# Computing each weight strip's low half in two GpSimd operations of 128x512 instead of one of 128x1024

## What is computed

```
h = h + mixed @ w_out                              # mixed: hyena long convolution and mLSTM
h = h + cross_attention(rms_norm(h), rms_norm(mem), wq, wk, wv, wo)
h = h + square(relu(rms_norm(h) @ ff_w1)) @ ff_w2
...
b_a, c_a, x_a, x_b, g_b, ga, gb = split(rmsnorm(x) @ w_in)
y_a = b_a * causal_conv(c_a * x_a);  y_b = rg_lru(causal_conv(x_b)) * gelu(g_b)
x = x + (sigmoid(ga) * (y_a @ w_out_a) + sigmoid(gb) * (y_b @ w_out_b)) @ w_o
x = x + (silu(h @ w_gate) * (h @ w_up)) @ w_down;  return rmsnorm(x)
```

## Time and profile before

| | |
|---|---|
| median of 3 runs | 1944.73 us (1944.62 to 1947.07) |
| the profiled execution: time, span | 1949.02 us, 1947.2 us |
| busy: PE, DVE, POOL, ACT | 1776.1, 1055.6, 753.2, 584.5 us |
| mean granted TensorE clock | 0.956 of full speed |
| weight strips | 302, 512 KB each |

### The profile page before, as it was taken

One profiled execution on the slowest core, in us unless ns is written; L12 is line 12 of the kernel. 1 busy time (PEld: TensorE's weight loads), 2 busy tenths in 40 slices (PEclk: granted clock), 3 DMA queues, 4 the chain that ended last, 5 costly groups with the idle time before them and its releaser, 6 DMA issues.

```text
span 1947.2 us, 21967 instructions
## 1 busy us (share of the span) xinstructions
PE 1776.1 (91%) x7718; PEld 1433.0 (74%) x7718; DVE 1055.6 (54%) x1379; ACT 584.5 (30%) x709; POOL 753.2 (39%) x312
## 2 busy tenths in 40 slices
PE   6799988975889998999999789898999999999996
PEld 4677876654667677888888577676888888888885
DVE  5751487879782566233248867575533463133137
ACT  2322332332212221111111254646433233122221
POOL 3432441113333143444444244444544444444442
PEclk9899998987899998999999899999999999999998
DMA  4232220110222022222222122223222222222222
GB/s 156 87 109 76 96 78 33 44 44 32 87 97 76 33 92 71 97 97 97 97 97 97 65 87 93 102 86 104 91 97 97 97 95 96 94 95 96 97 97 97
DMA packets 47694, 169.28 MB, mean 87 GB/s; under 512 B 5204, under 2 KB 5204, under 8 KB 47320
## 3 DMA queue, kind: packets, MB, share of 16 engines
q1 hardware_dynamic: 44640, 160.45, 23.6%
q10 hardware_dynamic: 3000, 8.09, 1.2%
HBM read 166.43 MB, written 2.10 MB: 87 GB/s over the span
## 4 chain that ended last, share of the span: by engine, by line
issue 31%; PE 29%; POOL 13%; DVE 1%; POOLq 0%; ACT 0%; DVEq 0%
POOL m_w_lo L433 13%; PE ps L465 10%; PE ps L467 10%; PE ps L466 10%; DVE m_h L1917 0%; DVE m_s L1187 0%; POOLq L441 0%; POOLq L439 0%; POOL m_QL L453 0%; DVE m_qs L1559 0%; PE ps L493 0%; DVE m_qs L1561 0%; DVE m_s L1894 0%; DVE m_ftmp L1551 0%; DVE m_ftmp L1549 0%
## 5 line engine op out<-in xcount | busy, mean ns | idle before, releaser
L433 POOL TENSOR_TENSOR m_w_lo<-m_raw,m_w_hi 128x1024 fp32r<-128x1024 f32 x302 | 738.8, 2450 | 1119.1 <-ACT m_w_hi L875 1119.1
L875 ACT ACTIVATE m_w_hi<-m_raw 128x1024 fp32r<-128x1024 f32 x302 | 317.7, 1056 | 761.4 <-DMA m_raw<-in_strips 757.6
L465 PE MATMUL ps<-m_XH,m_w_hi 128*128 128x512 f32 x1160 | 474.4, 409 | 36.6 <-POOL m_w_lo L433 22.5
L466 PE MATMUL ps<-m_XL,m_w_hi 128*128 128x512 f32 x1160 | 458.8, 396 | 0.0
L467 PE MATMUL ps<-m_XH,m_w_lo 128*128 128x512 f32 x1160 | 458.6, 395 | 0.0
L465 PEld LDWEIGHTS ps<-m_XH,m_w_hi 128*128 128x128 f32 x1160 | 222.7, 192 | 101.0 <-POOL m_w_lo L433 27.2
L466 PEld LDWEIGHTS ps<-m_XL,m_w_hi 128*128 128x128 f32 x1160 | 223.0, 192 | 47.6 <-issue 2.7
L467 PEld LDWEIGHTS ps<-m_XH,m_w_lo 128*128 128x128 f32 x1160 | 222.0, 191 | 47.9
L465 PE MATMUL ps<-m_FH,m_w_hi 128*128 128x512 f32 x432 | 168.9, 391 | 3.3 <-DVE m_FL L1180 3.2
L466 PE MATMUL ps<-m_FL,m_w_hi 128*128 128x512 f32 x432 | 168.6, 390 | 0.0
L467 PE MATMUL ps<-m_FH,m_w_lo 128*128 128x512 f32 x432 | 168.5, 390 | 0.0
(11 more groups left out here) (311 smaller groups left out, 2295.8 us busy)
## 6 DMA issues: line engine op xcount, KB each, us to landing
m_raw<-in_strips SPq DMA_DIRECT2D x302, 512.0 KB, 3.2
m_x_in<-in_x ACTq DMA_DIRECT2D x8, 256.0 KB, 4.6
m_x_res<-in_x ACTq DMA_DIRECT2D x1, 2048.0 KB, 8.0
out<-m_h SPq DMA_DIRECT2D x8, 256.0 KB, 2.1
m_memf<-in_mem ACTq DMA_DIRECT2D x1, 1024.0 KB, 10.4
m_decay<-in_decay ACTq DMA_DIRECT2D x1, 1024.0 KB, 15.1
m_w<-in_w ACTq DMA_DIRECT2D x1, 512.0 KB, 13.6
m_skip<-in_skip ACTq DMA_DIRECT2D x1, 512.0 KB, 3.9
```

Of the source, the lines that this page charges most:

```text
L433: nc.gpsimd.tensor_tensor(w_lo[:, c], raw[:, c], f(w_hi[:, c]), ALU.subtract).then_inc(lo_ready, 1)
L465: pe.matmul(dst, w_hi[:, c], xh, start=first, stop=False)
L466: pe.matmul(dst, w_hi[:, c], xl, start=False, stop=False)
L875: act.activation(w_hi[:, c], raw[:, c], ACT.Copy).then_inc(hi_ready, 1)
```

## The change

`low` runs over the two halves of a strip, and each half adds one to `lo_ready`. Every wait on `lo_ready` on TensorE is doubled, so that TensorE still starts a strip when the whole of it is there. ACT, DVE and SP are unchanged, and so are the six operations on `QL`.

```diff
             def low(slot):
-                c = slice(slot * STRIP, (slot + 1) * STRIP)
-                nc.gpsimd.tensor_tensor(w_lo[:, c], raw[:, c], f(w_hi[:, c]), ALU.subtract).then_inc(lo_ready, 1)
+                for part in range(2):
+                    c = slice(slot * STRIP + part * (STRIP // 2), slot * STRIP + (part + 1) * (STRIP // 2))
+                    nc.gpsimd.tensor_tensor(w_lo[:, c], raw[:, c], f(w_hi[:, c]), ALU.subtract).then_inc(lo_ready, 1)
...
             def strip(n, slot, bank, xh, xl, kt=KT, taken=None, needs=None, counts=None, width=T):
 
-                pe.wait_ge(lo_ready, n + 1)
+                pe.wait_ge(lo_ready, (n + 1) * 2)
...
                     n = v * 6 + 5
-                    pe.wait_ge(lo_ready, i * 12 + (S_IN + n + 1))
+                    pe.wait_ge(lo_ready, (i * 12 + (S_IN + n + 1)) * 2)
```

More of the change, by code:

```diff
@@ L716, in _ @@
             for u in range(4):
-                pe.wait_ge(lo_ready, S_WOUT + u + 1)
+                pe.wait_ge(lo_ready, (S_WOUT + u + 1) * 2)
                 for k in range(4, KT):
```

## The result

The changed kernel takes 1912.18 us (median of 4 runs, 1910.67 to 1914.59), the kernel before 1944.67 in runs on the same chip. The ratio is 0.9831, with a 95% interval of 0.9814 to 0.9848: 1.7% faster, 32.5 us. The forecast was 1933 (11.6 us less), with a range from 1928 to 1948. The sign was right and the gain was almost three times the forecast one.

What follows compares the result with a forecast made beforehand. PE, busy 1776.1 of 1947.2 us, was taken as the bound, not POOL; the change halves POOL's port lock on DVE. Terms summed to -11.55 from the median 1944.73, giving 1933.2 (forecast 1933), range 1928 to 1948.

Steps and rivals of the forecast that it cites:

- Rival C: Everywhere: POOL keeps the port between halves, so DVE waits as before and d longer; 1949.3 us, chance 0.12.
- Rival B: Gains are given back as POOL's second half takes the port first; two places remain, 1943 us, chance 0.19.
- Rival D: in_turn: strip C's low sets the turn, which grows by 0.59 us; 1944 to 1949 us, chance 0.07.
- d: Fixed extra time of two halves over one whole POOL operation: taken as 0.12 us, bounds 0 to 0.25.
- The taps at 112.71: PE's 4.56 us wait for L1256, held by the second of two low; released after its first half: -1.0 us.
- the three mLSTM units: L1422 released 1.1 us earlier, PSUM reads next, about 0.3 lost on L1440: 3 x 0.8 = -2.4 us.
- the Hyena block of `L1561`: A half-length block of L1561 ahead of PE's 2.81 us wait at 460.04: -1.1 us.
- the residual: After w_out, 541 to 580: L1197 released earlier at three places followed by PSUM reads: 3 x 0.9 = -2.7 us.
- the last residual: Before PE's 3.98 us wait at 1073.97: last tile's L1180 released 1.1 earlier, and 0.3 before that: -1.4 us.
- the first hidden chunk: 740 to 765: L1178 held less, mostly given back to L1180, inside PE's 3.18 us wait: -1.7 us.
- the second half delays strip C's `low` by 0.6: in_turn replay: taps let go 1.1 us earlier, but the turn gains only 0.08, 8 turns: -0.6 us.
- What it gives back, place by place: List of gains from hand replays of held DVE operations; from -0.6 us in in_turn to -2.7 after w_out.

Runs made afterwards that it cites:

- Experiment 5: Kernel before, with one strip in six of each in_turn turn in halves, beside the first pair of taps: 1944.01 us, ratio 0.9973.
- experiment 6: Kernel before, with only the fourth strip of each in_turn turn in halves, beside the scan: 1952.38 us, ratio 1.0009.
- experiment 4: Changed kernel, but TensorE starts a strip at the first half's signal and waits for the second ahead of the fifth block: 1915.23 us, ratio 0.9845.
- Experiment 7: Kernel before, whole operations, with 64 extra throwaway matmuls on TensorE in the Hyena part's wait between its two orders: 1987.75 us, ratio 1.0200.
- experiment 1: Kernel before, with halves only for the 48 strips of in_turn, whole operations elsewhere: 1931.76 us, ratio 0.9911.
- hi first: TensorE does w_hi matmuls first, waiting for POOL only before a strip's last eight: four parts 1889.04 us against 1882.36, eight parts 1859.51 against 1870.61.

## Why the prediction was wrong in size

**What bounds the kernel, and the mechanism: right.** The two stretches in which TensorE is never short moved by +0.2 and +1.5 us. One detail of the readings is off: a held operation does not end when POOL's does, but later by about its own work, 0.55 us for the tap (1181.40 against 1180.85) and 1.1 for the scan. Rival C, a port kept between the halves, has fallen with the first row of DVE: 2.45 for the pair of taps. Rival B, everything given back, fell with the result; the give-back exists, at the places named (`L1852` 1.60, and `L1718` and `L1720`, six blocks of 1.2 as foretold), but it is not the rule. Rival D has fallen too: the turn got shorter. Rival B was close at single places: what the scan gained was given back all but 0.1 a turn.

**d: about right, and without weight.** In the same stage a whole strip took 2.40 and two halves 2.54, so d is 0.14, against my 0.12, and each further part added 0.14 as well. The Trainium skill, page "GPSIMD Engine Reference" (section 3.1), led to an estimate of 0.18; what the traces show lies between the two, nearer to 0.12. The 42 places at which d was to be paid had no weight: POOL's busy time grew by 75 us, and eight parts, which add 1.0 us a strip, were faster still.

**Single places: right where I looked.** The taps at 112.71 gave 1.08 (forecast 1.0), the three mLSTM units 0.6, 1.0 and 0.8 (2.4 in sum, forecast 2.4), the Hyena block of `L1561` 1.1 (1.1), the residual 2.9 (2.7), the last residual 1.3 (1.4), the first hidden chunk 1.5 (1.7). These are shifts between the same operation in the two traces. Of the four waits of PE that the prediction names as signs two moved about as said (4.56 to 3.74 at 112.71, forecast 3.5; 3.18 to 1.67 at 765.05, forecast 1.5). Ahead of 579.75 the wait stayed (2.37 to 2.56, forecast near 0): PE came to it as much earlier, and the gain lay in its two smaller waits before, 1.63 to 0 and 2.57 to 1.80. Ahead of 1073.97 it fell further than forecast (3.98 to 0.86, not 2.6), and the next wait, at 1079.45, took 1.9 of that back.

**The step that failed first: in_turn, "the second half delays strip C's `low` by 0.6, which PE's slack before it doesn't all cover ... So 0.08 a turn".** The `low` of strip C did take 0.6 us longer (2.83 before, 3.46 with halves). But it began 1.0 us earlier in its turn, since ACT's copy ahead of it came earlier too, and it ended 12.5 us after the turn's `pX` instead of 12.9, in every one of the turns. In the turn from 1167.98 PE waited 0.34 us for it before, and not at all in its counterpart after.

The replay also let the gain at the taps die at ACT, in the slack of 0.5 that rival D names. That slack is the time from the landing of a load, at about 1182.7, to ACT's copy at 1183.30. But this load is the next strip's, copied at 1191.94; the copy at 1183.30 uses the load before it, issued at 1173.36 and landed 3.2 us later, with 6.8 us of slack (3.9 us at least in the other turns). Loads and copies come in the same order, so the pairing can be counted. The two loads and the copy, before:

```profile
1173.36 0.33 SPq L416 DMA_DIRECT2D m_raw<-in_strips  x1
...
1179.37 0.33 SPq L416 DMA_DIRECT2D m_raw<-in_strips  x1
```

```profile
1182.76 0.63 ACT L1126 ACTIVATE m_AH<-m_yA 128x512 fp32r<-128x512 f32 x1 [5.03 <-DVE m_yA L1829]
1183.30 1.04 ACT L875 ACTIVATE m_w_hi<-m_raw 128x1024 fp32r<-128x1024 f32 x1
```

In the changed kernel this is seen directly: ACT's copy at 1152.52 starts 1.66 after the issue at 1150.86, and the loads of this stage took 3.2 us and more to land, so it uses another one.

```profile
1151.98 0.63 ACT L1127 ACTIVATE m_AH<-m_yA 128x512 fp32r<-128x512 f32 x1 [4.22 <-DVE m_yA L1830]
1152.52 1.04 ACT L876 ACTIVATE m_w_hi<-m_raw 128x1024 fp32r<-128x1024 f32 x1
```

```profile
1150.86 0.33 SPq L416 DMA_DIRECT2D m_raw<-in_strips  x1
```

What ends a turn is the chain of DVE and ACT by itself. Over `in_turn` DVE waited for ACT for 86.2 us, before and after, and for TensorE for 0.3; ACT waited for DVE alone, 120.5 us before and 106.1 after. PE's waits in the turn are the effect: they are for POOL's `low` (the longest 2.84 us before, 1.92 after), and that `low` waits for ACT's copy behind the gates. So what the chain gains, the turn gains.

The two blocks at the taps are shorter by 1.1 us each, and both are followed by operations that read PSUM (`L1813`, `L1827`). About 0.5 of the 2.2 is given back at the next SBUF operations, `L1816` (0.93 instead of 0.69) and `L1830` (1.07 instead of 0.69). From `pX` to the end of ACT's `AH` it is 15.41 us before and 13.74 after, 1.67 less, and 0.15 less in the rest of the turn, 1.82 a turn. Experiment 5 shows the first of the two blocks by itself (0.97 a turn), experiment 6 the scan (0.1), experiment 4 that the wait for POOL doesn't count; the second block was not run by itself. Of what the replay said of the turn, the lengths were right (taps let go 1.1 earlier, `low` of strip C 0.6 longer, scan given back); what was wrong is what they end in.

**The second: "What it gives back, place by place" counted DVE's places and not TensorE's clock.** In the mLSTM part the blocks that I did list gave what I said. Others of the same kind were not listed: `L1344` beside two `low` (1.0), `L1440` (0.6), `L1442` (1.1). And 3.2 us of the 9.5 are PE's busy time, for the same matmuls. Timelines of PE, before and changed, at the same operation:

```profile
310.81 2.07 PE L629 MATMUL ps<-m_gM,m_sel 4*128 4x512 f32 x2 [2.34 <-DVE m_s L1413]
...
313.40 0.63 PE L466 MATMUL ps<-m_XL,m_w_hi 128*128 128x512 f32 x1
```

```profile
307.83 1.12 PE L630 MATMUL ps<-m_gM,m_sel 4*128 4x512 f32 x2 [1.35 <-DVE m_s L1414]
...
309.22 0.39 PE L467 MATMUL ps<-m_XL,m_w_hi 128*128 128x512 f32 x1
```

After a wait of 2.34 two matmuls took 2.07, and those behind them 0.63, at a granted clock of 0.50 (310.8 to 313); after one of 1.35 they took 1.12 and 0.39, at 1.00 (307.8 to 309.2). A wait that is 1 us shorter gave 2.5 us within the next 4. The same is seen at 367.86 and 395.83. It is no rule: at 112.71 and 340.00 the waits were shorter by 0.8 and 0.6 and the clock higher behind them, but the 0.8 to 1 us of this were lost again within 6 us, when the clock fell later instead. Experiment 7 shows the clock's part in the second order of the Hyena part, 2.5 us of 3.4; in the mLSTM part it is read from the traces and was not isolated.

**What stays open.** Why the Hyena part with the same halves gains anything from 2.5 to 5.2 us. Matmul by matmul, PE's idle time there is nearly the same in all four kernels (between 0.7 less and 0.9 more than before), and its busy time is 2.7 to 5.1 us less; the kernel of experiment 1, with whole operations there, had 2.3 us less busy and 1.8 more idle. So the scatter is in the clock, and what sets it there is not shown. Open is also how the difference of 38.1 in the profiled pair and 32.5 in the medians divides over the stages, and why `hi first` cost time outside `in_turn` at four parts.

## What to carry to other kernels

An operation that holds something exclusively costs the others its length, not its share of time. Cut it, and let the fixed part of each piece (here 0.14 us, on an engine that is 39% busy) be paid by the idle engine. In this kernel a piece of 1.25 us still took back much of what it gave an operation of 0.7, and pieces of 0.7 and 0.42 took back less; how far to cut was found by running it, and the last cut only paid in full after TensorE's order was changed too. When a gain is replayed along a chain, check each link that would absorb it, a transfer above all, by counting which transfer the waiting instruction needs, not by which lands just before it. Where TensorE waits in short stretches, a shorter wait can be worth more than its length, since the clock behind it can be higher; here it was so at some places, and at others the gain was lost again, so look at the busy time of the same matmuls as well as at the idle time.

## What the runs showed of the hardware

- A `tensor_tensor` of POOL on 128 partitions took 2.40 us for 1024 columns, and 2.54, 2.82 and 3.40 for the same in two, four and eight operations.
- Between two POOL operations queued back to back one DVE operation got through. A chain of DVE operations on 128x8, 0.17 us each when alone, took 2.3, 1.2 and 0.66 us each beside POOL pieces of 128x1024, 128x512 and 128x256.
- A DVE operation that was held ended after the POOL operation by about its own work: 0.06 us on 128x8, 0.55 for a tap on 128x512, 1.1 for the scan.
- At full clock, matmuls of 128x512 in full float32 followed each other every 0.86 us (64 in 55.0), and those in the fast form every 0.23.
